# A hybrid encoder block on one Trainium2 core: the fronts of the token tiles start a period sooner, their scaling and picking are split, and two weight loads take other buffers

## The reference, cut to what matters

```python
n = rms_norm(h, g_mix)                      # h: 1024 tokens x 1024
gq, gk, gv, gz, gb, ga, sq, sk, sv = split(n @ w_in)
o_gdn = gated_delta_net(...)                # causal conv (4 taps) over 1536 channels, then 64-token chunks
o_swa = sliding_window_attention(...)       # window 128
h = h + concat(o_gdn, o_swa) @ w_out
# PEER: 8 heads; per head and token the 16 best of 128 x 128 product keys
xb = rms_norm(h, g_ffn);  qr = xb @ w_query;  s1, s2 = qr . keys1, qr . keys2
v1, i1 = top_k(s1, 16);  v2, i2 = top_k(s2, 16)
sc, ci = top_k(v1[:, None] + v2[None, :], 16)
eid = i1[ci // 16] * 128 + i2[ci % 16];  gate = softmax(sc)
h = h + sum_k gelu(expert_u[eid_k] . xb) * gate_k * expert_v[eid_k]
h = h + sigmoid(rms_norm(h, g_ple) @ w_gate) * (p @ w_proj)
```

## Time and profile before

| | us |
|---|---|
| runs on record | 3536.38, 3541.54, 3543.12 (median 3541.54) |
| the profiled execution, whole | 3535.6 |
| its span, first to last instruction | 3533.8 |
| PE busy | 2612.1 (74%) |
| DVE busy | 2230.6 (63%) |
| POOL busy | 2140.7 (61%) |
| ACT busy | 1168.4 (33%) |
| bytes moved by DMA | 1227.83 MB, mean 347 GB/s |

### The profile page before, as it was taken

One profiled execution on the slowest core, in us unless ns is written; L12 is line 12 of the kernel. 1 busy time (PEld: TensorE's weight loads), 2 busy tenths in 40 slices (PEclk: granted clock), 3 DMA queues, 4 the chain that ended last, 5 costly groups with the idle time before them and its releaser, 6 DMA issues.

```text
span 3533.8 us, 37536 instructions
## 1 busy us (share of the span) xinstructions
PE 2612.1 (74%) x10985; PEld 1196.8 (34%) x10985; DVE 2230.6 (63%) x7062; ACT 1168.4 (33%) x3412; POOL 2140.7 (61%) x2069
## 2 busy tenths in 40 slices
PE   7997896785678667775786587757775678557877
PEld 5653343431343224322532243214321343113332
DVE  3125574666766866586668666777677766845543
ACT  2321233422342234323342334233422342223332
POOL 2202353555777677767776677667776777667663
PEclk9998898997889789977998798879898889778888
DMA  8115687888999999999999999999999999999995
GB/s 299 59 47 203 235 318 260 310 317 327 375 396 391 387 387 397 391 389 394 390 396 406 371 401 387 405 382 402 396 394 385 386 397 392 391 388 388 376 370 210
DMA packets 377540, 1227.83 MB, mean 347 GB/s; under 512 B 36296, under 2 KB 63992, under 8 KB 377208
## 3 DMA queue, kind: packets, MB, share of 16 engines
q0 software_dynamic: 294912, 1073.87, 78.5%
q1 hardware_dynamic: 79368, 141.94, 10.9%
q10 hardware_dynamic: 3056, 9.63, 0.7%
HBM read 1203.08 MB, written 22.21 MB: 347 GB/s over the span
## 4 chain that ended last, share of the span: by engine, by line
PE 31%; DMA 18%; POOL 18%; issue 17%; DVE 11%; ACT 5%; SPq 0%; POOLq 0%; DVEq 0%; ACTq 0%
PE bank L1117 15%; PE expert_sum L1117 14%; DMA v_rows<-in_peer_v_dram,expert_id 13%; POOL u_rows L666 9%; POOL v_rows L675 9%; DVE u_rows L2018 4%; DMA u_rows<-in_peer_u_dram,expert_id 4%; PE bank L1120 2%; ACT L705 1%; ACT weight_diagonals L705 1%; DMA w_query<-in_w_in_dram 1%; DVE arena L1965 1%; DVE arena L1971 1%; DVE arena L1974 1%; ACT arena L705 1%
## 5 line engine op out<-in xcount | busy, mean ns | idle before, releaser
L1117 PE MATMUL expert_sum<-v_rows,weight_diagonals 128*64 128x512 f32 x4096 | 1194.4, 717 | 567.3 <-issue 429.2
L2018 DVE CUSTOM_DVE_ANT_0 u_rows<-u_rows,ffn_in 128x512 f32<-128x512 f32 x2048 | 1309.7, 687 | 355.2 <-DMA u_rows<-in_peer_u_dram,expert_id 353.6
L666 POOL DMA_INDIRECT u_rows<-in_peer_u_dram,expert_id x1024 | 1053.0, 1028 | 642.6 <-issue 387.8
L675 POOL DMA_INDIRECT v_rows<-in_peer_v_dram,expert_id x1024 | 1040.5, 1016 | 535.9 <-issue 288.9
L1117 PEld LDWEIGHTS expert_sum<-v_rows,weight_diagonals 128*64 128x64 f32 x4096 | 320.6, 156 | 1251.6 <-issue 1240.8
L1117 PE MATMUL bank<-w_query,arena 128*128 128x512 f32 x576 | 286.6, 647 | 34.0 <-DMA w_query<-in_peer_w_query_dram 33.0
L705 ACT ACTIVATE weight_diagonals<-constants,expert_weight 128x64 f32<-128x64 f32 x1024 | 272.4, 336 | 8.3
L1117 PE MATMUL bank<-arena 128*128 128x128 f32 (+4 forms) x2176 | 247.7, 284 | 25.7 <-DVE arena L1778 13.1
L1117 PEld LDWEIGHTS bank<-arena 128*128 128x128 f32 (+3 forms) x2176 | 231.1, 191 | 83.4 <-issue 51.5
L1117 PE MATMUL bank<-w_out_sb,arena 128*128 128x512 f32 x512 | 226.5, 599 | 9.8 <-ACT arena L1083 6.5
L1120 PE MATMUL bank<-constants,arena 128*128 128x128 f32 x952 | 151.1, 301 | 108.7 <-DVE arena L1818 35.9
(11 more groups left out here) (194 smaller groups left out, 2052.2 us busy)
## 6 DMA issues: line engine op xcount, KB each, us to landing
w_query<-in_peer_w_query_dram SPq DMA_DIRECT2D x64, 1024.0 KB, 12.2
u_rows<-in_peer_u_dram,expert_id POOLq DMA_INDIRECT x1024, 7.5
v_rows<-in_peer_v_dram,expert_id POOLq DMA_INDIRECT x1024, 7.5
w_out_sb<-in_w_out_dram SPq DMA_DIRECT2D x2, 4096.0 KB, 18.7
w_query<-in_w_in_dram SPq DMA_DIRECT2D x12, 512.0 KB, 7.9
conv_scratch<-w_query SPq DMA_DIRECT2D x12, 384.0 KB, 6.8
arena<-conv_scratch SPq DMA_DIRECT2D x6, 768.0 KB, 5.0
tok_scratch<-token_out ACTq DMA_DIRECT2D x7, 648.0 KB, 3.0
```

The source lines that it names most:

```text
L666: nc.gpsimd.indirect_dma_start(u_ring[:, j, :], None, table_u, bass.IndirectOffsetOnAxis(id_of(q, j), 0)).then_inc(u_landed[j], 16)
L675: nc.gpsimd.indirect_dma_start(v_ring[:, j, :], None, table_v, bass.IndirectOffsetOnAxis(id_of(q, j), 0)).then_inc(v_landed[j], 16)
L1117: return nc.tensor.matmul(out_, lhsT, rhs, start=start, stop=stop, **kw)
L2018: last = v.tensor_tensor_reduce(u_ring[:, j, half], u_ring[:, j, half], xb[:, j % NB, half], 1.0, 0.0, ALU.mult, ALU.add, hid_half[:, q % ...
```

## The change

1. **Order table.** `pieces` grows from 16 to 18 numbers. The scaling of the heads (`piece2` on DVE) becomes `scale_queries` (number 3: q, q times decay, v) and `scale_keys` (number 4, with `piece3`). Picking the first four heads becomes number 14, between `best_pair(1)` and `best_pair(2)`; `best_pair(3)` stands alone as number 16. For tiles 2 to 7 the front's number 1 now runs in the last period (g = 15) of the tile two before, numbers 0, 2 and 3 in g = 0, number 4 in g = 1, and number g + 3 in period g. The levels, norms and attention, and the first two best pairs so stand one period sooner than before; the last number stays at g = 14. Tile 1's front starts in the same period as before.
2. **fill.** `pick` lets up to six slots of dots through; `piece1` begins with four, `scale_keys` with two.
3. **`add_h1`** (PE puts the residual into `acc`) moves from inside the first expert sums of a tile to the start of period g = 1.
4. **Loads.** `channels(0)` and `channels(1)` read their weights from the last two slots of `v_ring`. SP issues `a_nT` and these two loads ahead of the last two `load_w_query`; the loads for tiles 2 and 3 follow these. POOL's last `v` pair of period 0 waits for `channels(1)`.
5. **Period 7** (q = 6): PE finishes the expert sums of the period before ahead of the front's transposes. The transposes and their ACT copies come in the order q, qg, k, kb, and the products wait for all four.

```diff
+            if e == 0 and g < NG - 1:
+                at = {5: (1, 2), 6: (0, 3, 4), 7: (5, 6), 8: (7,), 9: (8, 9), 10: (10, 11), 11: (12, 13), 12: (14, 15), 13: (16,),
+                      14: (17,)}
+                return [(1, i) for i in at.get(g, ())]
+            if g == NG - 1:
+                return [(e + 2, 1)] if e + 2 < NT else []
+            if e == NT - 1:
+                return []
+            return [(e + 1, 0), (e + 1, 2), (e + 1, 3)] if g == 0 else [(e + 1, g + 3)]
+
+        def late_w_channel(ct):
+
+            return v_ring[:, G - 2 + ct, :].rearrange("p (c n) -> p c n", n=P) if ct < 2 else a_wc[ct % 2]
...
             for i in range(2, NQ):
                 sp.wait_ge(query_mm, i - 1)
+                if i == NQ - 2:
+                    sp.wait_ge(h1_mm, 2)
+                    for u in range(2):
+                        sp.wait_ge(rows_stored[u], 16 * ((LT + u) // 2))
+                    sp.dma_start(a_nT, nT_dram.rearrange("t p (c n) -> p t c n", n=P)).then_inc(wch_loaded[2], 16)
+                    sp.wait_ge(a_tok_stored, 16 * LT)
+                    for ct in range(2):
+                        load_w_channel(ct)
                 load_w_query(i)
...
             def gather_v(q, pair):
+                if q == 0 and pair == PAIRS - 1:
+                    pool.wait_ge(a_channels_mm, channels_done(1, 1))
...
+            pieces = [piece0, piece1, decays_of, scale_queries, lambda t: (scale_keys(t), piece3(t)),
                       lambda t: (level(t, 1), level(t, 2)), lambda t: (level(t, 3), level(t, 4)),
...
-                      lambda t: None, lambda t: best_pair(t, 0), lambda t: best_pair(t, 1), lambda t: best_pair(t, 2),
-                      lambda t: (best_pair(t, 3), pick(t, 0, 4)), lambda t: (pick(t, 4, 4), gates(t, 0, PH, vector_front))]
+                      lambda t: None, lambda t: best_pair(t, 0), lambda t: best_pair(t, 1), lambda t: pick(t, 0, 4),
+                      lambda t: best_pair(t, 2), lambda t: best_pair(t, 3),
+                      lambda t: (pick(t, 4, 4), gates(t, 0, PH, vector_front))]
...
+                if q % NG == 1:
+                    add_h1(t - 1)
                 for ct in channel_tiles(q):
                     channels(ct)
                 if q % NG == NG - 1:
                     rows_to_pairs(t)
-                for i in front_piece(q):
-                    pieces[i](t)
+                if q == CHANNEL_PERIODS:
+                    finish_slots()
+                for e, i in front_piece(q):
+                    pieces[i](e)
```

More of the change, by code:

```diff
@@ L561, in _ @@
             sp.wait_ge(query_mm, NQ - 1)
-            for ct in range(2):
+            for ct in range(2, 4):
                 load_w_channel(ct)
@@ L854, in piece2 @@
                     act.wait_ge(rel_stored, 16)
[L855 removed]
+                for i, (dst, b) in enumerate(((qnT, 5), (qgT, 0), (knT, 3), (nkbT, 4))):
                     fill(1)
@@ L1020, in _ @@
             first, rest, whole = slice(0, EARLY * G), slice(EARLY * G, SLOTS), slice(0, SLOTS)
-            for piece in pieces[:10]:
+            for piece in pieces[:11]:
                 piece(0)
@@ L1216, in channels @@
                     for c in range(DC):
-                        last = mm(bank[2 * u + half][:, 0:n * P].rearrange("p (t n) -> p t n", n=P), a_wc[u][:, c, :],
+                        last = mm(bank[2 * u + half][:, 0:n * P].rearrange("p (t n) -> p t n", n=P), late_w_channel(ct)[:, c, :],
                                   a_nT[:, t0:t0 + n, c, :], c == 0, c == DC - 1)
@@ L1480, in expert_slots @@
             def expert_slots(q):
-                t, g = divmod(q, NG)
-                if g == 0:
-                    add_h1(t)
+                g = q % NG
                 for pair in range(PAIRS):
@@ L1512, in _ @@
             first, rest, whole = slice(0, EARLY * G), slice(EARLY * G, SLOTS), slice(0, SLOTS)
-            for piece in pieces[:12]:
+            for piece in pieces[:13]:
                 piece(0)
@@ L1581, in _ @@
                 slots = expert_slots((NT - 1) * NG + g - 1)
+                if g == 1:
+                    add_h1(NT - 1)
                 finish_slots()
@@ L1687, in piece1 @@
             def piece1(t):
+                fill(4 if t > 1 else 0)
                 projected(dve, t, 1)
@@ L1735, in decays_of, with scaled_heads, scale_queries, scale_keys @@
                 dve.wait_ge(vector_step, steps(t))
[L1737 to L1749 removed]
+            def scaled_heads(t, items):
+                for dst, src, factor, need in items:
+                    if need:
+                        dve.wait_ge(scaled, 7 * t + need)
+                    v.tensor_tensor(heads(dst), heads(src), per_head(factor), ALU.mult).then_inc(scaled, 1)
+            def scale_queries(t):
+                dve.wait_ge(qkv_tok, 3 * t + 3)
+                dve.wait_ge(decays, t + 1)
+                fill(1)
+                scaled_heads(t, ((qn, bank[0][:, :], rst[:, 0:NH], 0), (qg, qn, eg, 1), (vb, bank[2][:, :], beta, 0)))
+            def scale_keys(t):
+                fill(2 if t > 1 else 0)
+                dve.wait_ge(h1_added, t)
+                scaled_heads(t, ((kn, bank[1][:, :], rst[:, NH:2 * NH], 0), (nkb, kn, nbeta, 4), (nkbg, nkb, eg, 5), (kdec, kn, kd, 4)))
             def level_mask(l):
@@ L2075, in _ @@
                     gates(0, 2, PH, vector_front)
-                for i in front_piece(q):
-                    pieces[i](q // NG + 1)
+                for e, i in front_piece(q):
+                    pieces[i](e)
                 fill(G)
```

56 lines of the change are left out of this document (17 added, 39 removed).

## The result

The changed kernel takes **3554.82 us** (median of 6 runs, 3551.2 to 3558.26), beside 3540.31 us (3535.2 to 3547.25) for the kernel before: ratio 1.0039, 95% interval 1.0023 to 1.0054. It is slower by 14 us (8 to 19), where 3529 us, 12 less than before, was forecast, and it lies 1.8 us above the stated range.

The account below looks back on a forecast made before the run. DMA was taken to bound steady tiles, PE's wait for channel weights the start. Terms +13 - 3 - 2 - 20 = -12 us took the profiled 3535.6 to 3523.6; 5.9 more for the median gave 3529 us, range 3514 to 3543.

Parts of the forecast that it names:

- A: Loads at the start: the last query loads queue behind the others, so PE's channels begin later; +13 us.
- R1: Rival at the start: query loads do not queue behind the others; A is -19, time 3497 us; chance 0.12.
- B: Period 7: with PE's sums ahead of the transposes, the products start about 3 us sooner; -3 us.
- C: Tile 0's picking: the overlong period is shared between two, only fills in the last pick free something; -2 us.
- D: Steady tiles 1 to 6: both u waits of g = 14 go, 3.4 us a tile; -20 us.
- R3: Rival: the steady gain stays out because the dips are paid elsewhere; D = 0, time 3549 us; chance 0.16.
- R4: Rival: DVE's new g = 0 chain delays the first u pair of g = 2; 3557 us; chance 0.16.

Follow-up runs that it names:

- e5: The changed kernel with the early loads undone and four dots instead of two ahead of the keys' scaling; 3522.1 us, 0.9947 of the kernel before.
- e3: The changed kernel with the early loads and the new order of q and k transposes and copies both undone; 3549.2 us, 1.0028 of the kernel before.

## Why the prediction was wrong

**A, loads: right.** +13 was said, +13.0 measured from the first gather to that of period 7, and 11 to 14 where A alone differs. The fourth query pair started at 374.55 and the channels at 388.26, that is 369 and 383 without P's 5.3, against 366.5 and 382. The reason given held: the queue has the same bytes to move either way, one packet for each of the gathers' (1388 against 1391 after), and putting the small packets first only chose which product waits. R1 is out.

**B, period 7: right within what can be told.** -3 was forecast, the two traces read -1.9, and alone on the kernel before they read -4.4. The `v` wait went as predicted, and the products started 2.9 us sooner. What took part of it back is not only the late copies, which the bound foresaw (PE still waited 0.77 us for ACT's last copy), but the granted clock: at 0.57 the products took 4.61 us for 2.82, and no term had that.

**C, tile 0's picking: not tested.** The two traces read -1.8 for -2, but kernels with this same code read 228.9 to 234.5 in that stage, around the 230.7 of before, so the agreement may be luck. No run tests it alone.

**D, steady tiles: the step that failed.** The gain side was right in kind, and with the rows let through also in size (15 to 20 us): both `u` waits of g = 14 went and the dip with them. The failed step is "I expect a short new wait there in exchange for the one before in g = 2", at no price. The wait came at the fourth `u` pair of g = 2, the same place in every tile, because DVE in g = 1 had to do the keys' scaling and the first inverse step around its last dots. The wait of up to 4.5 us outlasted the gathers still under way: it cost (2244.3 - 2220.5) / 6 = 4.0 us a tile, 24 in all, and (1.02 - 0.69) x 10 = 3.3 us of that is in one window. The tail was looked for in g = 0, where POOL covers it; g = 1 was never added up. This is R3 by its outcome (D = +4 for 0) and nearly R4 by its mechanism, one period later than R4 put it and decided by two dots rather than by a tail of 12 us.

**P, missed:** +5.3 ahead of the first gather. The order of q and k was weighed for period 7 and the steady tiles, where other work runs beside it, and never for tile 0's own front, where nothing does. The traces show it at 375 against 369 us; its share of the final time is not resolved.

Sum: -12 was forecast against the profiled execution; +20.8 came. The gap of 33 is D (24), P (5), B and C (1), and the 2 behind the last gather, as these two traces read. With two dots added the changed kernel stands at 0.9991 of before, -3 us (-7 to +1) where -12 was forecast; P may be part of what is still missing, the rest isn't located. The best version run is e5: the loads as before, everything else changed, four rows ahead of the keys: 0.9947 of before.

## What to carry to other kernels

When work is moved into a period whose engine lets transfers out between its steps, count after which step each pair of buffers comes free, not how busy the period is: two dots in the wrong place cost 24 us, and what was good in the change (the spread picking, q ahead of k) did not show until they were moved. Price a new wait by how long the gathers under way will last. An order that is free in the steady part must be costed again where the same code runs with nothing beside it, and loads that share a queue and its bandwidth can't all be early: say which one becomes late.

## What was not expected of the hardware

After PE had waited 3.99 us at 100 us, the granted clock read 0.50 for the next 8 us, the lower level (1.2 GHz of 2.4), though PE was busy throughout, and 32 products that had taken 2.82 us took 5.10. In e3 waits of 3.08 us at 86 and 2.21 at 105 preceded a mean of 0.58 in 108 to 112; with 1.16 and 2.21 at the same places, before, it stayed at 1.00. The products behind these waits took 2.28 us longer in the one case (for 3.99 us of wait) and 1.70 in the other, about half of the wait again. The clock took 1.8 us in period 7 as well, where the sums had been moved away from between the transposes. And on DVE 2.2 us of waiting for PE (3.16 for 0.97) went with about 4 us a tile, because the last dots, and with them POOL's next pair, stood behind that wait.
